# Sixteen gate tiles and 22 attention slots: Sigmoid as Tanh at half the argument, and slots between inner steps

## What is computed

```python
h = rmsnorm(x, n1) * (1 + sc1) + sh1
q, k, v, gb, gcv, u, ga, gv = split_proj(h @ w_in)
y_attn = windowed_attention(q, k, v, kc, vc, sink) @ w_attn_out
y_conv = conv_branch(gb, gcv, u, conv_w, w_conv_out)
x = x + g1 * ((sigmoid(ga) * y_attn + sigmoid(gv) * y_conv) @ w_mix_out)
```

## Time and profile before

| | us |
|---|---|
| median of 3 runs | 3140.84 (3139.32 to 3143.69) |
| the profiled execution | 3152.67 |
| its span | 3150.8 |
| PE busy in the span | 2792.7 (89%) |
| DVE busy | 2102.3 (67%) |
| ACT busy | 1292.2 (41%) |
| POOL busy | 621.2 (20%) |
| gate tiles with slots 12 to 27 | 221.35 to 361.44 |
| slots 28 to 33 | 361.44 to 394.85 |
| branch and mix | 394.85 to 487 |

### The profile page before, as it was taken

How to read it: one execution, slowest core, us unless ns; L and a number is a source line. 1 busy time by engine, 2 the same in 40 slices (tenths; PEclk the granted TensorE clock), 3 DMA queues, 4 the chain that set the end, 5 groups by cost and what they waited for, 6 DMA issues and landing times. The chain is left out here.

```text
span 3150.8 us, 41247 instructions
## 1 busy us (share of the span) xinstructions
PE 2792.7 (89%) x14404; PEld 2085.8 (66%) x14404; DVE 2102.3 (67%) x4568; ACT 1292.2 (41%) x2937; POOL 621.2 (20%) x531
## 2 busy tenths in 40 slices
PE   6999898887888888589898999788899999989998
PEld 6777777732344443245565777446888989978998
DVE  6784454398878776684687566864536576665787
ACT  3336523344344344464453222353443443433444
POOL 0000000144444445333232233331000000000000
PEclk9999899999999999789898899889899999999999
DMA  6531122499999999899799899985432445533454
GB/s 235 210 126 61 47 74 87 172 420 421 421 420 420 421 417 412 341 354 418 300 414 392 337 417 417 406 317 225 161 127 88 146 146 182 181 112 136 134 182 141
DMA packets 155399, 822.34 MB, mean 261 GB/s; under 512 B 16448, under 2 KB 21696, under 8 KB 89408
## 3 DMA queue, kind: packets, MB, share of 16 engines
q0 software_dynamic: 73728, 536.90, 41.7%
q1 hardware_dynamic: 75792, 263.46, 24.1%
q10 hardware_dynamic: 5680, 19.40, 1.7%
HBM read 817.60 MB, written 2.10 MB: 260 GB/s over the span
## 5 line engine op out<-in xcount | busy, mean ns | idle before, releaser
L678 POOL DMA_INDIRECT slots<-in_experts,consts x312 | 371.1, 1189 | 1205.9 <-DVE consts L2282 581.5
L2305 DVE SCALAR_TENSOR_TENSOR slots<-slots,work 128x1024 f32<-128x1024 f32 x312 | 382.1, 1225 | 91.9 <-DMA slots<-in_experts,consts 79.9
L980 PE MATMUL psum<-slots,acc 128*128 128x512 f32 x652 | 316.6, 629 | 72.0 <-ACT acc L1596 71.8
L1930 DVE TENSOR_TENSOR wlo<-w,whi 128x1024 fp32r<-128x1024 f32 x259 | 314.6, 1220 | 96.3 <-ACT whi L1391 95.4
L1391 ACT ACTIVATE whi<-w 128x1024 fp32r<-128x1024 f32 x259 | 272.3, 1052 | 153.8 <-PE psum L726 146.3
L980 PEld LDWEIGHTS psum<-slots,acc 128*128 128x128 f32 x652 | 124.4, 198 | 249.9 <-issue 131.9
L1584 ACT ACTIVATE consts<-consts 128x1 f32<-128x1 f32 x512 | 101.1, 197 | 378.6 <-DVE slots L2305 219.4
L711 PE MATMUL psum<-xres,w 128*128 128x256 f32 x1040 | 242.6, 390 | 0.0
L678 POOL DMA_INDIRECT split_slots<-in_experts,consts x148 | 185.2, 1251 | 257.9 <-issue 95.3
L711 PEld LDWEIGHTS psum<-xres,w 128*128 128x128 f32 x1040 | 200.0, 195 | 50.4 <-issue 23.5
L2305 DVE SCALAR_TENSOR_TENSOR split_slots<-split_slots,work 128x1024 f32<-128x1024 f32 x148 | 181.2, 1225 | 42.9 <-DMA split_slots<-in_experts,consts 36.7
(11 more groups left out here) (361 smaller groups left out, 6034.4 us busy)
## 6 DMA issues: line engine op xcount, KB each, us to landing
w<-in_stream SPq DMA_DIRECT2D x408, 512.0 KB
back_w<-in_back SPq DMA_DIRECT2D x64, 512.0 KB, 4.5
arena<-in_wmod SPq DMA_DIRECT2D x4, 2048.0 KB, 17.8
arena<-in_wmod ACTq DMA_DIRECT2D x8, 1024.0 KB, 6.0
acc<-in_wmod ACTq DMA_DIRECT2D x8, 1024.0 KB, 7.9
slots<-in_experts,consts POOLq DMA_INDIRECT x312
split_slots<-in_experts,consts POOLq DMA_INDIRECT x148
xres<-in_xT SPq DMA_DIRECT2D x1, 2048.0 KB, 14.9
```

Source lines behind the costliest of these rows:

```text
L678: pool.indirect_dma_start(out=slots[slot], out_offset=None, in_=a["experts"], in_offset=bass.IndirectOffsetOnAxis(ap=indices[:, p:p + 1], ...
L980: mm = pe.matmul(bank(6 + half), diag(p), v[:, half * T:(half + 1) * T], start=(c == 0), stop=(c == PICKS - 1))
L1930: dve.tensor_tensor(wlo[:, s, :, :].rearrange("p k n -> p (k n)"), w32[:, s, :], whi[:, s, :, :].rearrange("p k n -> p (k n)").bitcast(F32 ...
L2305: dve.scalar_tensor_tensor(u, u, 1.0, tokens[:, p // PICKS, :], ALU.mult, ALU.mult, accum_out=inner[:, c:c + 1]).then_inc(sem("dotted"), 1)
```

## The change

The six slots of the tail and the sixteen behind the gate tiles are put between steps inside the gate tiles: `gate_plan` deals 22 slots over the first 120 of 128 steps, so that five or six steps lie between two slots. The last tile has no slot behind or inside it. The pairs that it makes are (slot, steps of the tile done ahead of it): tile 0: (12, 5); tile 1: (13, 2), (14, 8); tile 2: (15, 5); tile 3: (16, 3), (17, 8); tile 4: (18, 6); tile 5: (19, 3); tile 6: (20, 1), (21, 6); tile 7: (22, 4); tile 8: (23, 1), (24, 6); tile 9: (25, 4); tile 10: (26, 1), (27, 7); tile 11: (28, 4); tile 12: (29, 2), (30, 7); tile 13: (31, 5); tile 14: (32, 2), (33, 8); tile 15: none.

The gate is no longer sigmoid(z) but tanh(z / 2), with sigmoid(z) = (1 + tanh(z / 2)) / 2. DVE adds the 1 in the branch stage, in one three-operand instruction with the product, and the half goes into g1 once, ahead of slot 12.

```diff
+GATES, GATE_SLOTS = 16, range(12, 34)
+def gate_plan():
+    outs, behind, done = [], [], 0
+    for i in range(GATES):
+        outs.append(("gate", i))
+        at = []
+        while done < len(GATE_SLOTS) and (done + 1) * (KB * GATES - 8) // len(GATE_SLOTS) <= KB * (i + 1):
+            at.append((GATE_SLOTS[done], (done + 1) * (KB * GATES - 8) // len(GATE_SLOTS) - KB * i))
+            outs.append(("value", GATE_SLOTS[done] - 2))
+            done += 1
+        behind.append(at)
+    return outs, behind
...
-    section("gates", [1, -1] * 16)
-    section("tail", [-1] * 6)
+    section("gates", [1 if kind == "gate" else -1 for kind, _ in GATE_OUTS])
...
             n, o = SECTIONS["gates"]
-            for i in range(16):
-                linear(n + i, o + 2 * i)
-                attn_slot(12 + i)
-            for i in range(28, 34):
-                attn_slot(i)
+            for i in range(GATES):
+                wait_tile(pe, n + i)
+                wait_bank(pe, gate_out(i))
+                dst, s, begun = out_bank(gate_out(i)), (n + i) % RING, 0
+                for slot, steps in SLOTS_BEHIND[i] + [(None, KB)]:
+                    for k in range(begun, steps):
+                        pe.matmul(dst, whi[:, s, k, :], XH(k), start=(k == 0), stop=False)
+                        pe.matmul(dst, whi[:, s, k, :], XL(k), start=False, stop=False)
+                        mm = pe.matmul(dst, wlo[:, s, k, :], XH(k), start=False, stop=(k == KB - 1))
+                        if k == KB - 1:
+                            mm.then_inc(tile_done, 1)
+                    begun = steps
+                    if slot is not None:
+                        attn_slot(slot)
...
-            for i in range(16):
+            for i in range(GATES):
                 dst = acc[:, i // 2, :] if i % 2 == 0 else gv[:, i // 2, :]
-                copy_product(dst, o + 2 * i, func=ACT.Sigmoid)
-                attn_slot(12 + i)
+                for slot, steps in SLOTS_BEHIND[i]:
+                    if steps < KB:
+                        attn_slot(slot)
+                copy_product(dst, gate_out(i), func=ACT.Tanh, scale=0.5)
+                for slot, steps in SLOTS_BEHIND[i]:
+                    if steps == KB:
+                        attn_slot(slot)
                 upper_after(n + i)
-            for i in range(28, 34):
-                attn_slot(i)
...
+            step(dve.tensor_scalar(mod[:, 16:24, 0], mod[:, 16:24, 0], 0.5, None, ALU.mult))
             gain_of(2, 32, 0, "n2")
-            for i in range(12, 34):
-                attn_slot(i)
-                if i < 28:
-                    lower_after(first_tile("gates") + i - 12)
+            step.settle()
+            for i in range(GATES):
+                for slot, _ in SLOTS_BEHIND[i]:
+                    attn_slot(slot)
+                lower_after(first_tile("gates") + i)
...
-                    free(dve.tensor_tensor(t, out_bank(o + 2 * m + j), t, ALU.mult), o + 2 * m + j)
+                    free(dve.scalar_tensor_tensor(t, t, 1.0, out_bank(o + 2 * m + j), ALU.add, ALU.mult), o + 2 * m + j)
```

More of the change, by code:

```diff
@@ L61 @@
 NCONST = _at
+GATES, GATE_SLOTS = 16, range(12, 34)
[10 more added lines that the diff above has]
+    return outs, behind
+GATE_OUTS, SLOTS_BEHIND = gate_plan()
 def plan():
@@ L494, in attn_product, with gate_out @@
                 return SECTIONS[f"conv{u + 2}"][1] + 1
-            return SECTIONS["gates"][1] + 2 * (u - 10) + 1 if u < 26 else SECTIONS["tail"][1] + u - 26
+            return SECTIONS["gates"][1] + GATE_OUTS.index(("value", u))
+        def gate_out(i):
+            return SECTIONS["gates"][1] + GATE_OUTS.index(("gate", i))
         def x_half_value_out(i, h):
@@ L2185, in _ @@
                 for j, t in ((0, acc[:, m, :]), (1, gv[:, m, :])):
-                    wait_read(dve, SECTIONS["gates"][1] + 4 * m + 2 * j)
+                    wait_read(dve, gate_out(2 * m + j))
                     wait_product(dve, o + 2 * m + j)
-                    free(dve.tensor_tensor(t, out_bank(o + 2 * m + j), t, ALU.mult), o + 2 * m + j)
+                    free(dve.scalar_tensor_tensor(t, t, 1.0, out_bank(o + 2 * m + j), ALU.add, ALU.mult), o + 2 * m + j)
                     wait_read(dve, o + 2 * m + j)
```

## The result

The changed kernel takes 3126.23 us (median of 13 runs), the kernel of before 3145.97 (13 runs): 19.7 us less. The ratio of the runs is 0.9939 with a 95% interval of 0.9926 to 0.9952, so between 15 and 23 us less. The profiled execution's span is 3118.1 us. First its page: span and clock row, which answers to the earlier trace rows.

What follows compares the result with a forecast made beforehand. PE was taken to bound the gate stage and a chain of latencies the six-slot tail. 17.6 (tail) + 2.4 (clock) - 0.2 (stall) = 19.8 us off the median 3140.84 gave 3121.0 us, range 3113 to 3131.

Steps and rivals of the forecast that it cites:

- The sum: Whole kernel: 17.6 + 2.4 - 0.2 = 19.8 us less, 0.63% faster, at 3121.0 us; chance 0.82.
- Part 1: Tail behind the last gate tile: six slots moved between steps cost 15.83 us instead of 33.41, gain 17.6 us.
- Part 2: Branch's first four steps: PE arrives without idle time, so the clock stays up; gain 2.4 us, low bound 0.
- Part 3: Gate stage: 32 table loads, 41 us of ACT time, go; worth 0 us alone, but said to make Part 1 possible.
- Part 4: Dealt slots in the gate tiles: a loop of 4.5 us fits the spacing of 6.66 or 7.36 us.
- The term of 0.2 us for slot 13: Slot 13's turning, with DVE late out of the convolution: a stall of 0 to 0.5 us, taken as 0.2.
- its worst place: Slots 19 to 21, where gate 5 ends late and slot 20 comes early: margin 1.3 us, no stall.
- Part 5: Branch: 16 three-operand products cost DVE 1 us more, 0.12 of it in PE's path, covered by 2.0: 0 us.
- Stalls: Rival in the closer slots: a loop of 7.5 us makes 20 slots lose some 0.5 each, 3131 us; chance 0.09.
- Not arriving: Rival after the stage: something there runs by a transfer, so the time would be 3140.8 us; chance 0.04.
- The slower rival: Gate stage: the clock falls under denser slots; a third at 1.2 GHz costs 42 us, giving 3163; chance 0.05.
- The signs: Profile checks: gate 0 to branch 155 to 157 us, clock 1.00, later stages the same within some 5 us.

Runs made afterwards that it cites:

- second profile of before: The kernel of before, unedited, profiled once more: 173.21 us from gate tile 0 to the branch, against 173.50 in its first profile.
- The two kernels with slots put back: Changed kernel with slots 32 and 33, or slots 30 to 33, put back behind gate tile 15: gate 0 to branch 157.46 and 165.03 us.
- 96 steps: Changed kernel with the 22 slots dealt over the first 96 of 128 steps instead of 120: gate 0 to branch 156.12 us.
- with 72: Changed kernel (Tanh) with the 22 slots dealt over the first 72 steps instead of 120: gate 0 to branch 160.38 us.
- 48 steps: Changed kernel with the 22 slots dealt over the first 48 steps instead of 120: gate 0 to branch 172.06 us.
- Sigmoid kernel of 72 steps: Changed kernel with Sigmoid, old g1 and two-operand product, slots dealt over the first 72 steps: gate 0 to branch 168.48 us.
- second pair: Second profiles of the kernel of before and the changed kernel, both unedited: spans 3141.1 and 3119.8 us.
- four-slot kernel: Changed kernel with slots 30 to 33 put back behind gate tile 15: gate 0 to branch 165.03 us.

## Why the prediction was right, point by point

**The sum** was 19.8 us, for 0.63%; measured 19.7 us by the medians, 0.61% by the ratio. With an interval of 15 to 23 us the close agreement of the totals is in part luck. What bears the prediction out is the stage. Its working held within 0.1 us: it gave 33.41 to 15.83 for the six slots, and the stage became 17.60 shorter. The clock behind it gave 2.46 for 2.4.

**Part 1 had two causes under one number.** The 33.41 us of the tail are 15.8 of work at full clock (155.90 - 140.09), 9.4 of waits (3.00, 0.29, 1.74, 2.65, 0.75 and 0.98 on PE's timeline), and so 8.2 us that the lower clock added to the work. With the 2.46 at the branch that is 10.6 of 20.1 us. The prediction booked only the 2.4 as the clock's. But 8.2 is a way of booking, and not what a full clock would have given back, since PE then waits longer: in the second profile of before the loop from turning to turning took 375.45 - 370.86 = 4.59 us at clock 1.00, 1.61 of it a wait, and with Tanh alone 379.56 - 374.95 = 4.61. Four such loops are 18.4 us against the 23.2 from 365.59 to 388.80, so an estimate from these rows is 4.8 us for the clock in that stretch and 2.46 at the branch, 7.3 of the 20.1, with the last 6 us of the tail left out. The sum came out because it priced the moved slots at full clock. The two kernels with slots put back show both parts apart: 1.7 us of waits at full clock for two slots, waits and clock for four.

**Part 2**, no idle time to fall in: right, clock 1.00 into the branch.

**Part 3 was wrong in its last sentence.** The loads are off PE's path, as it said. But they are not "what makes part 1 possible": with Sigmoid the dealt slots took 156.52 us. Nor was Tanh by itself worth 0 in the old order: one load stood in the tail, at 362.3, outside the stretch that the prediction cites for PE not waiting, and without it the first wait was 1.4 us shorter. The sum doesn't hang on that, as the tail goes whole. The prediction's own part 4 had the numbers for it, 4.5 + 1.3 = 5.8 us under 6.66, and did not draw the conclusion. What the runs put in its place: Tanh is worth 0.6 us at five or six steps between slots and 8.1 at three or four.

**Part 4**, margins: right that nothing stalls. The loop of 4.5 us was 4.59 in the second profile of before, at clock 1.00. It was worked out from a tail that the prediction took to be at half clock throughout; behind the turning of 376.84 it was not (1.00 in 380 to 382). The term of 0.2 us for slot 13 was 0.0, with 1.14 us to spare. For slot 21, its worst place, it gave 1.3 us, and the trace shows 2.05. The tightest place is one that it didn't name, slot 32 with 0.92; Sigmoid's only wait was there too. Closer together, slot 13 comes first among the waits that matter: 0.26 with 96 steps, 1.37 with 72.

**Part 5**: hidden, right; the three-operand product took 0.678 to 0.689 us and the two-operand one 0.684 to 0.692, so it costs nothing more, not 0.06.

**The rivals.** Stalls: none at this spacing, real at 72 and 48 steps. Not arriving: the mix output, the keys' scores and the expert sums begin 20.1 to 20.2 us earlier in the changed kernel's first profile (the sums at 605.1 for 625.2); it arrived whole. The slower rival, that the clock falls in the denser stage, did not occur: 1.00 in both profiles. At 48 steps it fell, in and behind waits of PE within slot work, and cost up to 4.6 us; that is the mechanism of the rival in small, though no fall was seen there without a wait ahead of it. Which waits bring the clock down is open: 1.60 us at 230.8 in the 48-step kernel did, 2.75 us at 322.5 with the Sigmoid kernel of 72 steps did not (clock 1.00 in 325.30 to 330).

**The signs.** From the branch's fifth step to the end the time was to stay the same within some 5 us. It was 12.6 us less in the first pair of profiles (2738.1 for 2750.7), so this sign failed there; in the second pair it held (2740.1 for 2741.5).

**The range**, 3113 to 3131, held 3126.23. The point, 3121.0, was 5 us low, not by the change but by its base: the three runs shown of the kernel of before have a median of 3140.84, and 13 runs have 3145.97.

## What to carry to other kernels

A chain of small steps that waits on other engines costs little if each is put between pieces of the bound engine's own long work, and a lot if the last few stand alone: six slots cost 33.4 us in a row and 15.8 between steps. Before moving them, compare the loop from one to the next (here 4.6 us as measured, some 5.9 with a table load as an estimate from its 1.28) with the spacing on hand, and check the first place, where the other engines come late out of the stage ahead. Work that is taken off an engine which nobody waits for, as 31 table loads here, is worth little until the spacing is one where the loop no longer fits (0.6 us at five or six steps, 8.1 at three or four), so test the two edits apart.

## What the runs showed of the hardware that was not expected

A tail of four slots with 1.74 us of wait in it lost the clock within its first waiting slot, and one of two slots with waits of 0.75 and 0.97 did not. Once down, the clock stayed at 0.50 from 376 to 392 in the four-slot kernel, over slots and waits into the branch product. It doesn't always stay: with Tanh alone it went back to 1.00 at about 383.3, inside PE's wait of 2.65 us that ended at 385.56, and fell again at 386.7. In two profiles of the one kernel of before it was 0.50 and 1.00 in the same 6 us. A `scalar_tensor_tensor` with one operand from PSUM and an immediate took 0.678 to 0.689 us for 128 by 512 float32, as `tensor_tensor` on the same operands (0.684 to 0.692); the one of the mix product, with a per-partition scalar and other operands, took 0.75.
